# Gated DeltaNet scan: norms, gate rows and the first decays placed between slabs of the projection, the meta tokens' small inverse reordered

## Chip, cores and metric

The kernel runs on one core of a Trainium2 chip. The metric is the device time of one execution in microseconds, as the median of several runs.

## Reference

Two transformer blocks over a sequence of 256 tokens of width 1024, in f32. The first block puts 16 meta tokens (and 112 masked pads) ahead of the sequence and has two layers, of which the first mixes with a gated delta network. The change touches only the following part of it:

- `qkv = silu(conv4(h @ w_qkv))`: a projection to 4096 columns (8 heads of q, 8 of k, 16 of v, 128 each), a causal depthwise convolution of 4 taps, then silu.
- q and k are divided by their l2 norms per head and token: `q * rsqrt(sum(q*q) + eps)`, with a scale of 128^-0.5 for q.
- `beta = sigmoid(...)` and `g = -exp(a_log) * softplus(... + dt_bias)` give a gate per head (16) and token; `G` is the running sum of g inside a chunk.
- For each chunk and head a lower triangular matrix `A = beta * exp(G_i - G_j) * (k_i . k_j)` is inverted (I + A), giving the corrected values; the state S is carried from chunk to chunk, and outputs are `q S * exp(G)` plus a masked `(q_i . k_j)` part.

The kernel takes the 16 meta tokens as a first short chunk (the pads are zero), and the 256 others as two chunks of 128.

## The kernel before

Activations lie features first (128 features by T = 272 tokens, or 256). Weights stream from memory in slabs of 128 x 2048 words into a ring of four, and each slab is split by ACT (`w_hi`, L294) and DVE (`w_lo`, L297) into a high and a low part, two slabs ahead of use; PE makes three fast products per weight block (L411, L412, L413). Each engine has a program of its own, in order; semaphores join them. `each_product` writes ACT's and DVE's part of a streamed phase. It makes a hardware loop of four slabs, unless it is given `between`, a function called ahead of each slab, in which case the phase is written out straight; `stream_pe` does the same on PE. `late` with `lag=2` is work done two output parts behind.

The phase `gdn_qkv` has 16 slabs of two output parts (32 parts of 128 columns). For part u ACT copies the bank twice (L753, and L754 scaled by the last tap), DVE adds the three other taps (L769), and ACT applies silu two parts later (L759). A slab's split is called at its second part, ahead of that part's taps.

Around it stand, in the order of the programs:

- `rows_act`/`rows_dve`, ahead of the projection: the rows beta, G, exp(G) and others, 16 heads on 16 partitions. `rows_pe` (L732) turns them into columns, `cols_dve` copies them (L739, L740) into `colv` and `colb`. Both come after the projection.
- The norms, after the projection: ACT squares q and k in one instruction (L571, 16 heads by 272 tokens), PE sums over the features by 16 products with a one-column mask (L598, two passes each, so 32 records), ACT takes the root (L582), DVE the reciprocal (L587), and POOL sends the rows to memory (L815) and fetches them back on all partitions (L817 for the 16 meta tokens, L933 for a group of heads). The gate rows go the same way (L807, L811, L929).
- `first_dve`, `first_act`, `first_pe`, `first_pool`: the meta tokens' chunk for all 16 heads. DVE normalizes k and q (L830, L831) and makes the decays (L832, L834, exp on ACT L866, L836); PE makes k.k and k.q (L886, L887) and turns k and v (L890, L892); DVE makes A (L840), the masked attention (L841) and the first step of the inverse (L843, L845). Three levels double the block size: POOL masks A (L824), PE makes Y (L904), ACT copies it (L871), PE makes two products (L909, L912), DVE subtracts (L856, L858). Then PE makes the new values (L916), ACT copies them (L874), PE makes the outputs (L920) and after them the state (L923), which DVE and ACT copy to `St0` (L861, L879).
- `ahead_kn`, `ahead_diff` on DVE, `ahead_exp` on ACT, `ahead_beta` on POOL: the same preparation for the first group of four heads (L940, L941, L947, L951, L961, L968). Then `group_*` runs four times, once for each group of four heads, over the two chunks of 128; its first product is L1100, its A is L1007, and `first_turned` (L1116) is PE's first product that needs the result of the group's first DVE steps.

Of the kernel before, what the change touches and what calls it, by code (L numbers as in the profile page):

```python
# [192 lines left out]
def program(nc, x_t, meta_t, mem_t, positions, stream, consts, params, sg_w_t, sg_bias, out_t, counts):  # L193
    with ExitStack() as ctx:
# [415 lines left out]
        sqh = area(rows_at + 9 * T, 16, T)  # L610
# [22 lines left out]
        bc0 = area(2048, 64, META, of=spare)  # L633
# [7 lines left out]
        kn0, qn0 = (spare[:, 6144 + 128 * i:6144 + 128 * (i + 1)].rearrange("p (a b) -> p a b", b=META) for i in range(2))  # L641
# [105 lines left out]
        def qkv_act(act):  # L747
# [12 lines left out]
            each_product(act, "gdn_qkv", 1, project, ACT.Silu, split="hi", late=silu, lag=2)  # L760

        def qkv_dve(dve):
# [8 lines left out]
            each_product(dve, "gdn_qkv", 1, body, split="lo")  # L771
# [17 lines left out]
        def by2(v):  # L789

            return v.rearrange("p (a b) n -> p a b n", b=2)
# [10 lines left out]
        def first_pool(pool):  # L802
# [14 lines left out]
            pool.dma_start(bc0[:, 0:16, :], on_all(scratch, 0, (T, 16), (1, META))).then_inc(S.sem("first_rows_in"), 16)  # L817
            fetch_norm_rows(pool, 0)
# [6 lines left out]

        def first_dve(dve):
            inc = lambda ins, step=None: S.inc(ins, "first_dve", step)
            own = lambda: S.own(dve, "first_dve")
            dve.wait_ge(S.sem("first_rows_in"), 32)
            inc(dve.tensor_tensor(kn0, qkv[:, 8:16, 0:META], bc0[:, 8:16, :], ALU.mult))  # L830
            inc(dve.tensor_tensor(qn0, qkv[:, 0:8, 0:META], bc0[:, 0:8, :], ALU.mult), "kn")  # L831
            inc(dve.tensor_tensor(c0["dec"], bc0[0:META, 32:48, :], over(cn("causal")[0:META, 0:META], HV), ALU.add))  # L832
            own()
            inc(dve.tensor_tensor(c0["dec"], c0["dec"], down(colv[0:META, 0, 1, :], META), ALU.subtract), "diff")  # L834
            dve.wait_ge(*S.at("first_act", "dec"))
            inc(dve.tensor_tensor(c0["decb"], c0["dec"], bc0[0:META, 16:32, :], ALU.mult))  # L836
# [4 lines left out]
            inc(dve.tensor_tensor(by2(c0["attn"]), two(kq), by2(c0["dec"]), ALU.mult), "attn")  # L841
# [4 lines left out]
            dve.wait_ge(*S.at("first_pe", "tok"))  # L846
            for b in range(2):
                kt = two(tile4(ps[b][0:META, :]))
# [1890 lines left out]
```

## Time and profile before

| | |
|---|---|
| median of 3 runs | 1789.52 us (1786.73 to 1790.91) |
| the profiled execution | 1782.2 us, span 1780.5 us |
| mean granted TensorE clock | 0.957 of full |
| busy share of the span | PE 92%, DVE 61%, ACT 46%, POOL 23% |
| projection `gdn_qkv` on PE | 29.0 to 126.3 us |
| first group starts on PE (L1100) | 196.87 us |

Times inside the profile are microseconds from the span's start. PE is the matrix engine and PEld its weight loads, DVE the vector engine, ACT the scalar engine, POOL GpSimd. "Busy" of PE includes records that overlap. The granted clock is a fraction of full speed; it takes two levels here, 0.50 (1.2 GHz) and 1.00 (2.4 GHz), and a stretch shows the mean. "Idle before <- X" names what ended an engine's wait.

### The profile page before, as it was taken

The page shows a single profiled execution, that of the slowest core. Times are in us where ns is not written, and L with a number is a line of the kernel's source. Part 1 is how long each engine was busy: PE and PEld are TensorE (multiplying, and loading weights), DVE is VectorE, ACT ScalarE, POOL GpSimd, SP SyncE. Part 2 cuts the span into 40 slices and gives each one's busy share as a digit, 9 for nine tenths or more (in the row PEclk, how much of TensorE's full clock was granted, in tenths as well). Part 3 has the DMA queues.
Part 4 walks back from the last instruction along what each step waited for, and adds up shares of the span by engine and source line. Part 5 has one row for each costly group of instructions (what it writes and reads, how often), then busy time and mean ns, then how long its engine had stood idle before and what let it go on. Part 6 is the DMA issues. An engine that isn't in the chain of part 4 may idle for free.

```text
span 1780.5 us, 32196 instructions
## 1 busy us (share of the span) xinstructions
PE 1640.7 (92%) x12819; PEld 1555.6 (87%) x12819; DVE 1085.1 (61%) x1519; ACT 827.2 (46%) x1190; POOL 408.4 (23%) x388
## 2 busy tenths in 40 slices
PE   5986888989889999899899998999999899889998
PEld 4984788878889999898899998999988489889998
DVE  4872355535558883575588846665563756566654
ACT  5661344445445544555555545433443145554332
POOL 0001344430024562000246513321100000212210
PEclk9996699999899999999999999999999999999999
DMA  5542011105335544363244455554633443445543
GB/s 216 186 143 62 4 47 50 51 1 193 137 123 169 186 140 154 124 235 119 72 170 185 145 169 193 197 179 147 234 126 119 162 147 119 137 151 202 196 155 128
DMA packets 41400, 252.40 MB, mean 142 GB/s; under 512 B 4480, under 2 KB 6640, under 8 KB 19296
## 3 DMA queue, kind: packets, MB, share of 16 engines
q1 hardware_dynamic: 37376, 233.13, 37.7%
q0 software_dynamic: 3936, 18.05, 3.3%
q8 instruction: 61, 1.00, 0.2%
q14 instruction: 27, 0.22, 0.0%
HBM read 249.99 MB, written 1.17 MB: 141 GB/s over the span
## 4 chain that ended last, share of the span: by engine, by line
PE 81%; DVE 10%; ACT 5%; issue 2%; DMA 1%; POOL 0%; SPq 0%; ACTq 0%; DVEq 0%; POOLq 0%
PE bank L411 20%; PE bank L412 20%; PE bank L413 20%; DVE w_lo L297 3%; PE bank L1124 2%; PE bank L1132 2%; PE bank L415 2%; PE bank L598 2%; ACT w_hi L294 2%; PE bank L542 1%; PE bank L429 1%; PE bank L1139 1%; PE bank L430 1%; PE bank L431 1%; DVE rs L551 1%
## 5 line engine op out<-in xcount | busy, mean ns | idle before, releaser
L411 PE MATMUL bank<-work_r,w_hi 128*128 128x256 f32 (+2 forms) x3264 | 932.5, 286 | 29.9 <-DVE w_lo L297 16.4
L412 PE MATMUL bank<-work_r,w_hi 128*128 128x256 f32 (+2 forms) x3264 | 926.2, 284 | 0.0
L413 PE MATMUL bank<-work_r,w_lo 128*128 128x256 f32 (+2 forms) x3264 | 925.8, 284 | 0.0
L297 DVE TENSOR_TENSOR w_lo<-ring,w_hi 128x2048 fp32r<-128x2048 f32 (+2 forms) x233 | 497.9, 2139 | 331.6 <-ACT w_hi L294 331.5
L411 PEld LDWEIGHTS bank<-work_r,w_hi 128*128 128x128 f32 x3264 | 622.9, 191 | 35.8 <-DVE w_lo L297 22.5
L294 ACT ACTIVATE w_hi<-ring 128x2048 fp32r<-128x2048 f32 (+2 forms) x233 | 408.1, 1754 | 470.6 <-PE bank L413 470.5
L412 PEld LDWEIGHTS bank<-work_r,w_hi 128*128 128x128 f32 x3264 | 622.4, 191 | 0.5
L413 PEld LDWEIGHTS bank<-work_r,w_lo 128*128 128x128 f32 x3264 | 622.1, 191 | 0.0
L1326 POOL TENSOR_TENSOR work<-work 128x272 f32<-128x272 f32 (+1 forms) x44 | 91.6, 2082 | 137.0 <-ACT work L1289 137.0
L523 POOL TENSOR_TENSOR sq<-sq 128x256 f32<-128x256 f32 (+2 forms) x36 | 57.6, 1599 | 268.3 <-ACT sq L500 267.5
L1314 DVE SCALAR_TENSOR_TENSOR work<-work,params_sb 128x272 f32<-128x272 f32 (+1 forms) x176 | 99.8, 608 | 5.2 <-issue 0.2
L429 PE MATMUL bank<-work_r,w_hi 128*128 128x256 f32 (+2 forms) x112 | 41.7, 372 | 16.9 <-DVE work_r L1721 14.9
L1698 POOL CAST work_r<-mix 128x256 f32 (+1 forms) x44 | 17.5, 399 | 164.0 <-DVE mix L1689 164.0
L769 DVE SCALAR_TENSOR_TENSOR work<-work,params_sb 128x272 f32<-128x272 f32 x96 | 46.9, 500 | 10.6 <-ACT work L754 2.8
L1302 DVE TENSOR_TENSOR work<-bank,rs 128x272 f32<-128x272 f32 (+1 forms) x88 | 37.7, 431 | 24.8 <-PE bank L413 24.7
L1026 DVE TENSOR_TENSOR sq<-sq,bank 128x256 f32<-128x256 f32 x48 | 18.0, 417 | 51.5 <-PE bank L1132 51.5
L1282 ACT ACTIVATE work<-work,params_sb 128x272 f32<-128x272 f32 (+1 forms) x88 | 48.1, 595 | 1.3 <-DVE work L1302 1.2
L1710 ACT ACTIVATE work_r<-hs,params_sb 128x256 fp32r<-128x256 f32 (+2 forms) x48 | 24.6, 512 | 51.0 <-DVE hs L1742 21.8
L979 POOL TENSOR_TENSOR sq<-mix,consts_sb 128x512 f32<-128x512 f32 x24 | 33.6, 1400 | 46.1 <-PE bank L1124 28.8
L1330 POOL TENSOR_TENSOR work_r<-work,work_r 128x272 f32 (+3 forms) x44 | 40.1, 910 | 7.7 <-POOL work_r L1328 7.4
L429 PEld LDWEIGHTS bank<-work_r,w_hi 128*128 128x128 f32 x112 | 23.5, 210 | 19.9 <-issue 16.0
L1700 POOL TENSOR_TENSOR work_r<-mix,work_r 128x256 f32 (+1 forms) x44 | 37.5, 853 | 7.5 <-POOL work_r L1698 7.2
(410 smaller groups left out, 1900.9 us busy)
## 6 DMA issues: line engine op xcount, KB each, us to landing
ring<-in_stream SPq DMA_DIRECT2D x166, 1024.0 KB, 4.8
ring<-in_stream SPq DMA_DIRECT2D x64, 704.0 KB, 4.1
ring<-in_stream SPq DMA_DIRECT2D x10, 768.0 KB, 4.3
work<-rows_scratch POOLq DMA_DIRECT2D x4, 1632.0 KB, 7.9
work<-rows_scratch POOLq DMA_DIRECT2D x4, 544.0 KB, 8.7
work<-rows_scratch_o POOLq DMA_DIRECT2D x1, 2176.0 KB, 8.9
ring<-in_stream SPq DMA_DIRECT2D x3, 512.0 KB, 7.2
work<-rows_scratch_m POOLq DMA_DIRECT2D x1, 1088.0 KB, 8.1
```

The lines of the kernel that those rows point to most:

```text
L294: eng.activation(w_hi[:, slot, 0:size], raw_w, ACT.Copy).then_inc(hi_done, 1)
L297: eng.tensor_tensor(w_lo[:, slot, 0:size], raw_w, w_hi[:, slot, 0:size].bitcast(F32), ALU.subtract).then_inc(lo_done, 1)
L411: pe.matmul(out, w_hi[:, slot, at:at + P], hi, start=first, stop=False)
L412: pe.matmul(out, w_hi[:, slot, at:at + P], lo, start=False, stop=False)
L413: mm = pe.matmul(out, w_lo[:, slot, at:at + P], hi, start=False, stop=last)
L429: pe.matmul(out, w_hi[:, slot, at:at + P], hi, start=(k == 0), stop=False)
L523: S.inc(pool.tensor_tensor(sq[:, 0, 0:n], sq[:, 0, 0:n], sq[:, k, 0:n], ALU.add), "square_sums")
L769: S.inc(dve.scalar_tensor_tensor(out=y, in0=r[:, t:t + T], scalar=gdn_taps[:, un.u, t:t + 1], in1=y, op0=ALU.mult, op1=ALU.add), "qkv_dve")
L1282: S.inc(act.activation(y_gu[p2][:, m, 0:w], raw[p2][:, m, 2:w + 2], ACT.Identity, bias=bias[:, un.u, m:m + 1], scale=taps[:, un.u, m, 2:3] ...
L1314: S.inc(dve.scalar_tensor_tensor(out=y, in0=raw[p2][:, m, t:t + w], scalar=taps[:, un.u, m, t:t + 1], in1=y, op0=ALU.mult, op1=ALU.add), " ...
L1326: S.inc(pool.tensor_tensor(h, silu_g[un.j % 2][:, 0:w], y_gu[un.j % 2][:, 1, 0:w], ALU.mult), "up_pool")
L1330: S.inc(pool.tensor_tensor(lo[:, un.u, :], h, hi[:, un.u, :].bitcast(F32), ALU.subtract), "up_pool")
```

## The change

- Squares of q and k are made one head at a time by ACT inside the projection, one behind silu, and PE adds each pair of heads to the sum ahead of slabs 4 to 11. ACT takes the root ahead of slab 12, DVE the reciprocal ahead of slab 13; POOL sends and fetches the meta tokens' norm rows from there.
- The gate rows are turned by PE ahead of slab 3 and copied by DVE ahead of slab 4; the meta tokens' gate rows are fetched as soon as they are stored. The decays are made ahead of slabs 5 (difference), 6 (exp) and 7 (times beta); the normalized k and q of the meta tokens ahead of slab 15.
- `gdn_qkv` is given `between` on PE, ACT and DVE, so it is written out straight on the three.
- In the meta tokens' chunk, k and v are turned between the steps of the inverse, not ahead of it; the masked attention comes after the first step; the state is made ahead of the outputs. The first group's preparation is done ahead of the copies of the state, and PE starts the groups after ACT's copy of the outputs.
- Buffers are moved so that these live at the same time (`sqh`, `bc0`, `kn0`, `qn0`).

```diff
-                pe.wait_ge(S.sem("rown_squares"), (1, 2, 4)[use])
+                pe.wait_ge(S.sem("rown_squares"), (16, 17, 19)[use])
...
-        sqh = area(rows_at + 9 * T, 16, T)
+        sqh = area(8704 + 16 * T, 16, T)
...
-        bc0 = area(2048, 64, META, of=spare)
+        bc0 = sqw[:, 0:64 * META].rearrange("p (a b) -> p a b", b=META)
...
                 S.inc(act.activation(qkv[:, un.u, :], conv_y[:, un.j % 4, :], ACT.Silu), "qkv_act", "silu")
-            each_product(act, "gdn_qkv", 1, project, ACT.Silu, split="hi", late=silu, lag=2)
+                if 1 <= un.u <= 16:
+                    act.wait_ge(*S.at("qkv_act", turn=un.u - 1 + CONV_AHEAD))
+                    rown_squares(act, [(qkv[:, un.u - 1, :], sqh[:, un.u - 1, :])])
+
+            def beside(slab):
+                if slab == 6:
+                    first_decay_act(act)
+                elif slab == 12:
+                    rown_act(act, 0, [], T, 16, cn("l2_scale")[0:16, :], cn("l2_eps"), table=False)
+            each_product(act, "gdn_qkv", 1, project, split="hi", late=silu, lag=2, between=beside)
...
-            each_product(dve, "gdn_qkv", 1, body, split="lo")
+
+            def beside(slab):
+                if slab == 4:
+                    cols_dve(dve)
+                elif slab == 5:
+                    S.own(dve, "cols_dve")
+                    first_diff_dve(dve)
+                elif slab == 7:
+                    first_decay_dve(dve)
+                elif slab == 13:
+                    rown_dve(dve, 0, T, 16)
+                elif slab == 15:
+                    first_keys_dve(dve)
+            each_product(dve, "gdn_qkv", 1, body, split="lo", between=beside)
+
+        def qkv_pe(pe, slab):
+            if slab == 3:
+                rows_pe(pe)
+            for k in (2 * slab - 8, 2 * slab - 7) if 4 <= slab < 12 else ():
+                pe.wait_ge(S.sem("rown_squares"), k + 1)
+                mm = pe.matmul(ps[4][0:16, 0:T], cn("row_of", 15 - k, 16), sqh[:, k, :], start=(k == 0), stop=(k == 15))
+                if k == 15:
+                    S.begin("rown_pe")
+                    S.inc(mm, "rown_pe", "sums")
...
             pool.wait_ge(S.sem("scan_rows_out"), 48)
-            pool.wait_ge(*S.at("cols_dve"))
-            pool.wait_ge(*S.at("qkv_act", turn=31 + CONV_AHEAD))
             pool.dma_start(bc0[:, 16:64, :], on_all(scratch, 16 * T, (T, 48), (1, META))).then_inc(S.sem("first_rows_in"), 16)
-            fetch_gate_rows(pool, 0)
...
             pool.dma_start(bc0[:, 0:16, :], on_all(scratch, 0, (T, 16), (1, META))).then_inc(S.sem("first_rows_in"), 16)
+            pool.wait_ge(*S.at("cols_dve"))
+            pool.wait_ge(*S.at("qkv_act", turn=31 + CONV_AHEAD))
+            fetch_gate_rows(pool, 0)
             fetch_norm_rows(pool, 0)
...
+        def first_keys_dve(dve):
+            dve.wait_ge(S.sem("first_rows_in"), 32)
+            for u in (7, 15):
+                dve.wait_ge(*S.at("qkv_act", turn=u + CONV_AHEAD))
+            S.inc(dve.tensor_tensor(kn0, qkv[:, 8:16, 0:META], bc0[:, 8:16, :], ALU.mult), "first_dve")
+            S.inc(dve.tensor_tensor(qn0, qkv[:, 0:8, 0:META], bc0[:, 0:8, :], ALU.mult), "first_dve", "kn")
...
+                if l == 1:
+                    for b in range(2):
+                        kt = two(tile4(ps[b][0:META, :]))
+                        inc(dve.tensor_tensor(by2(ktl0[0:META, 8 * b:8 * b + 8, :]), kt, by2(down(colv[0:META, 0, 2, 8 * b:8 * b + 8], P)), ALU.mult),
+                            "ktl" if b else None)
+                    values(0)
+                elif l == 2:
+                    values(1)
+            ahead_kn(dve, 0)
+            ahead_diff(dve, 0)
             dve.wait_ge(*S.at("first_pe", "S"))
...
                 inc(mm, f"Y{l}")
+                if l == 1:
+                    keys()
+                elif l == 2:
+                    values(1)
...
                 inc(mm, f"XXT{l}")
+                if l == 1:
+                    values(0)
...
             pe.wait_ge(*S.at("first_act", "vn"))
             for h in range(HV):
+                mm = pe.matmul(ps[h // 4][:, h % 4 * P:(h % 4 + 1) * P], ktl0[0:META, h, :], vb0[0:META, h, :], start=True, stop=True)
+            inc(mm, "S")
+            for h in range(HV):
                 mm = pe.matmul(ps[6][:, h * META:(h + 1) * META], vb0[0:META, h, :], c0["attn"][:, h, :], start=True, stop=True)
             inc(mm, "o")
-            for h in range(HV):
-                mm = pe.matmul(ps[h // 4][:, h % 4 * P:(h % 4 + 1) * P], ktl0[0:META, h, :], vb0[0:META, h, :], start=True, stop=True)
-            inc(mm, "S")
...
             pe.wait_ge(*S.at("first_dve", "S"))
-            pe.wait_ge(*S.at("first_act", "S"))
+            pe.wait_ge(*S.at("first_act", "o"))
...
-            stream_pe(pe, "gdn_qkv", a_parts(0, T), T)
-            rows_pe(pe)
-            rown_pe(pe, 0, lambda k: sqh[:, k, :], 16, 1, T, 16)
+            stream_pe(pe, "gdn_qkv", a_parts(0, T), T, between=lambda slab: qkv_pe(pe, slab))
```

## Rows read from the trace of the kernel before

**Rows 1.** The page of the kernel before, its chain of waits by engine.

```profile
PE 81%; DVE 10%; ACT 5%; issue 2%; DMA 1%; POOL 0%; SPq 0%; ACTq 0%; DVEq 0%; POOLq 0%
```

**Rows 2.** Stretches: length, busy us (instructions) of PE, PEld, DVE, ACT, POOL, clock, DMA.

```profile
80.00:100.00 20.00, 20.00 (x164) 20.00 (x163) 17.32 (x24) 14.17 (x26) 0.00 (x0) 1.00 0.53 189
...
171.00:194.00 23.00, 20.88 (x96) 18.23 (x96) 0.00 (x0) 2.40 (x5) 0.00 (x0) 0.50 0.00 1
...
770.00:790.00 20.00, 20.00 (x164) 19.84 (x163) 10.80 (x15) 6.26 (x5) 1.66 (x3) 1.00 0.60 214
```

**Rows 3.** The chain of waits, 126 to 153 us: start, us, what.

```profile
126.44 0.40 ACT work L753
...
128.86 0.44 ACT work L759
...
133.20 9.60 PE bank L598 x32
...
142.82 0.58 ACT rrow L582
...
143.43 1.85 DVE rrow L587
```

**Rows 4.** The chain of waits, 147 to 205 us.

```profile
147.53 4.47 DMA w_spare<-rows_scratch
...
153.68 1.81 PE bank L890 x8
...
171.01 7.02 PE bank L916 x32
...
178.05 2.03 ACT work L874 x4
...
180.12 7.00 PE bank L920 x32
187.13 7.03 PE bank L923 x32
...
200.72 0.70 DVE mix L1007
...
204.19 0.67 PE bank L1116 x4
```

**Rows 5.** Timeline of ACT and DVE in mid projection: start, us, instruction, idle before.

```profile
84.92 1.92 ACT L294 ACTIVATE w_hi<-ring 128x2048 fp32r<-128x2048 f32 x1 [1.86 <-PE bank L413]
...
90.84 1.92 ACT L294 ACTIVATE w_hi<-ring 128x2048 fp32r<-128x2048 f32 x1 [1.86 <-PE bank L413]
...
104.63 2.29 DVE L297 TENSOR_TENSOR w_lo<-ring,w_hi 128x2048 fp32r<-128x2048 f32 x1 [0.22 <-ACT w_hi L294]
```

**Rows 6.** Groups by line in the projection: count, busy us, mean ns, idle before.

```profile
L769 DVE SCALAR_TENSOR_TENSOR work<-work,params_sb 128x272 f32<-128x272 f32 x95 | 46.4, 500 | 10.6 <-ACT work L754 2.8 <-DVE work L769 0.3 <-issue 0.2
...
L297 DVE TENSOR_TENSOR w_lo<-ring,w_hi 128x2048 fp32r<-128x2048 f32 x14 | 32.0, 2289 | 2.2 <-ACT w_hi L294 2.2
...
L759 ACT ACTIVATE work<-work 128x272 f32 x24 | 10.4, 432 | 0.0
...
L732 PE MATMUL bank<-consts_sb,work 16*128 16x16 f32 x8 | 0.6, 208 | 0.0
```

**Rows 7.** The norm sums of L598 alone, columns as in Rows 2.

```profile
138.00:142.00 4.00, 4.00 (x19) 1.71 (x18) 1.00 0.78 321
```

**Rows 8.** Timeline of all engines, 143 to 197 us.

```profile
143.41 1.28 ACT L1201 ACT_TABLE_LOAD   x1
...
144.71 1.06 ACT L956 ACTIVATE work<-work 128x1024 f32<-128x1024 f32 x1
...
154.29 0.41 DVE L840 TENSOR_TENSOR mix<-bank,mix 16x256 f32<-16x256 f32 x1
...
159.48 0.95 PE L904 MATMUL bank<-mix 16*16 16x16 f32 x32 [0.51 <-issue]
...
196.87 2.07 PE L1100 MATMUL bank<-work 128*128 128x128 f32 x8 [2.73 <-DVE work L941]
```

More of the change, by code:

```diff
@@ L640, in program @@
               for i, n in enumerate(("dec", "decb", "A0T", "attn", "X", "XT", "Am", "Y"))}
-        kn0, qn0 = (spare[:, 6144 + 128 * i:6144 + 128 * (i + 1)].rearrange("p (a b) -> p a b", b=META) for i in range(2))
+        kn0, qn0 = (sqw[:, 1024 + 128 * i:1024 + 128 * (i + 1)].rearrange("p (a b) -> p a b", b=META) for i in range(2))
         obc = area(8704, HV, T)
@@ L824, in first_pool, with first_diff_dve, first_decay_dve @@
                 inc(pool.tensor_tensor(c0["Am"], c0["A0T"], over(lvl[0:META, l, 0:META], HV), ALU.mult), f"Am{l}")
+        def first_diff_dve(dve):
+            dve.wait_ge(S.sem("first_rows_in"), 16)
+            S.inc(dve.tensor_tensor(c0["dec"], bc0[0:META, 32:48, :], over(cn("causal")[0:META, 0:META], HV), ALU.add), "first_dve")
+            S.own(dve, "first_dve")
+            S.inc(dve.tensor_tensor(c0["dec"], c0["dec"], down(colv[0:META, 0, 1, :], META), ALU.subtract), "first_dve", "diff")
+        def first_decay_dve(dve):
+            dve.wait_ge(*S.at("first_act", "dec"))
+            S.inc(dve.tensor_tensor(c0["decb"], c0["dec"], bc0[0:META, 16:32, :], ALU.mult), "first_dve", "decb")
+        def first_keys_dve(dve):
[4 more added lines that the diff above has]
+            S.inc(dve.tensor_tensor(qn0, qkv[:, 0:8, 0:META], bc0[:, 0:8, :], ALU.mult), "first_dve", "kn")
         def first_dve(dve):
@@ L828, in first_dve @@
             own = lambda: S.own(dve, "first_dve")
[L829 to L836, printed above, removed]
             own()
@@ L888, in first_pe, with keys, values @@
             inc(mm, "kq")
-            for h in range(HQ):
-                pe.transpose(ps[h // 4][0:META, h % 4 * P:(h % 4 + 1) * P], kn0[:, h, :], ident)
-            for h in range(HV):
-                mm = pe.transpose(ps[2 + h // 4][0:META, h % 4 * P:(h % 4 + 1) * P], qkv[:, 16 + h, 0:META], ident)
-            inc(mm, "tok")
+            def keys():
+                pe.wait_ge(*S.at("qkv_act", turn=31 + CONV_AHEAD))
+                for h in range(HQ):
+                    mm = pe.transpose(ps[h // 4][0:META, h % 4 * P:(h % 4 + 1) * P], kn0[:, h, :], ident)
+                inc(mm, "ktok")
+            def values(half):
+                for h in range(8 * half, 8 * half + 8):
+                    mm = pe.transpose(ps[2 + h // 4][0:META, h % 4 * P:(h % 4 + 1) * P], qkv[:, 16 + h, 0:META], ident)
+                inc(mm, f"vtok{half}")
             pe.wait_ge(*S.at("first_dve", "XT0"))
@@ L913, in first_pe @@
                 inc(mm, f"XXT{l}")
+                if l == 1:
+                    values(0)
             pe.wait_ge(*S.at("first_dve", f"XT{L0 - 1}"))
@@ L1193, in scan_dve @@
             first_dve(dve)
-            ahead_kn(dve, 0)
-            ahead_diff(dve, 0)
             with dve.Fori(0, GROUPS - 1) as g:
@@ L2401, in _ @@
             qkv_dve(dve)
-            cols_dve(dve)
-            rown_dve(dve, 0, T, 16)
-            S.own(dve, "cols_dve")
             scan_dve(dve)
```

28 lines of the change are left out of this document (13 added, 15 removed).

## Prediction

> **What bounds the kernel.** I read first the page's chain of waits. It runs over PE for 81% of the span [rows 1], so work on PE, and waits of PE, are what count. The stretches then show two kinds of time. In the projection PE is busy for all of its 20.00 us at clock 1.00, with DVE close behind at 17.32 [rows 2]. Between the end of the projection and the first group PE idles, or works at clock 0.50, as in 171 to 194 us [rows 2]. The chain tells who holds the end there. The last slab's last product ends near 126.3 us, ACT copies it from 126.44, and the last silu ends at 129.3 [rows 3]. Then squares, sums, root, reciprocal and a trip through memory follow one another until 152.0 [rows 3, 4]; the inverse leads to L916 at 171.01, and three blocks of about 7.0 us on PE with a copy of 2.03 between them end at 194.2. The first group's A starts at 200.72 and PE's first product behind it at 204.19 [rows 4]. Everything after 204.19 keeps its order, so the time gained is the move of that one product. I measure it from the projection's end, called E (126.3 before): it stands at E+77.9.
>
> **Part 1: the projection grows.** PE gets 16 sums of two passes. The old block has 32 records in 9.60 us [rows 3], part of it at half clock. At clock 1.00 it issues 18 loads in 4.00 us [rows 7], 0.22 each; 32 of them cost 7.2 us. The 12 small transposes, of which 8 take 0.6 us [rows 6], about 0.8 in all, stood behind E under ACT's and DVE's tail, and now lie on PE's path. Sum: 8.0 us.
>
> Is PE still the one that sets the pace? A slab lasts 5.92 us (84.92 to 90.84). Three slabs behind the first of these the w_hi at 102.68 starts as a slab ends (84.92 + 3 x 5.92); its w_lo starts at 104.63 and ends at 106.9; the slab that needs it starts at 102.6 + 5.92 = 108.5: 1.5 us to spare. ACT idles 1.86 us a slab, DVE 0.22 [rows 5]. DVE's own work is one w_lo of 2.29 and six taps of 0.50, some 5.6 with their gaps [rows 5, 6].
>
> In slabs 4 to 11 PE's two sums stretch the slab by 0.9 us. That gives DVE room for what it gets there: two differences and decb of 16x256 (0.41 each, as L840 in [rows 8]), and six copies of up to 128x48, which are smaller (estimate 0.7 in all, at most 6 x 0.41). It gives ACT room for two squares a slab (0.4 each, by L759 [rows 6]) and for exp with two table loads (0.41 + 2 x 1.28, the load by [rows 8]): I count ACT 1 us late at most in slab 6, inside the 1.5. Cost: 0.
>
> In slab 12 the stretching is over. Root and two loads cost ACT 0.58 + 2.56 = 3.1 us [rows 3, 8], against 1.86 idle; w_hi of slab 14 is 1.3 to 1.9 us late against 1.5 to spare, which just fits. Behind it the reciprocal, 1.85 us [rows 3], stands ahead of w_lo of the last slab, which also finds its second part's copies late. Following the three queues item by item, I get that w_lo ready 1.1 us after PE wants it. Taken: 1.1 us. The projection grows by 9.1 us. From below the growth is 8.0. From above, if everything given to ACT (16 x 0.4 + 1.0 + 4 x 1.28 = 12.5) and to DVE (0.7 + 1.2 + 1.85 + 0.5 = 4.3) came through, it is 8.0 + 16.8 = 24.8.
>
> The trace shows no pause around a table load: the one at 143.41 takes 1.28 us and the next instruction starts 0.02 us after it [rows 8]. The Trainium skill ("ScalarE: Activation LUTs", What ACT_TABLE_LOAD costs) adds a drain of about 1.38 us, 2.66 us in all for each switch of set, and tells the author to do all functions of one set together, which the new order does not. By that price each pair of loads costs 5.3 us, the last two splits come about 2.8 us later, and the gain shrinks from 18 to about 15. This trace does not agree with that price; the measured one is used.
>
> **Part 2: what goes from behind E.** Squares, sums, root, reciprocal, both trips and the normalizing leave the path. The norm rows now take 6.7 us (from the reciprocal's end at 145.28 to 152.0 [rows 3, 4]) beside the last slabs. Between the reciprocal and `first_keys` DVE has one w_lo and the taps of four parts, 2.2 + 4 x 1.7 = 9 us, so some 2 us are to spare. The gate rows have tens of us. DVE's last taps end 2.5 us behind E before; with the reciprocal and keys ahead of them I count 3.1. A of the meta tokens starts there, at E+3.1, where before it started at 154.29 [rows 8], E+28.0: 24.9 us gained.
>
> **Part 3: the inverse in its new order.** A, Y and XT take 1.3: E+4.4. PE's turn of X ends at E+5.0, but ACT has silu to E+3.55, the table load (1.28) and the v copy (1.06 [rows 8]) until E+5.9, so X is copied by 6.3. POOL issues two fetches behind that silu and has until 6.3 for them and the mask. Y1 at 6.35. From here eight turns of keys or values cost 1.8 us at half clock (L890 [rows 4]), and each small product block 1.0. PE's queue is then Y1, keys, XX1, XXT1, values, which ends at 12.9; Y2, values, XX2, XXT2 at 17.6; a subtraction (0.4), Y3, copy, XXT3, a subtraction: L916 at E+21.15. DVE's scalings of keys and values fit in those waits. From A to L916 is 18.05 us against 16.7 before (154.29 to 171.01): 1.3 lost, because the turns of values, once under the DVE steps, now stand between the levels. Bounds: 14.8 us if the turns hide (3.3 to Y1, and the 11.5 from L904 to L916 before [rows 4, 8]), 20.2 if all three add their 1.8 to that.
>
> **Part 4: outputs and state.** L916 to the end of the two blocks stays 23.2 us (171.01 to 194.18) in either order. PE then starts the group after ACT's copy of the outputs, 0.5, where it waited 2.7 before (194.18 to 196.87 [rows 8]) for DVE's copies and `ahead_kn`: 2.2 gained. The rest of the preparation is done by then, so A of the group waits for PE alone, and `first_turned` for PE's 6.0 us of products, where before DVE had it wait 7.3 (196.87 to 204.19): 1.4 gained. Bounds for both: 0 and 5. New position: 21.15 + 23.2 + 0.5 + 6.0 = E+50.8.
>
> **Sum.** 24.9 - 1.3 + 2.2 + 1.4 gives 27.1 behind E; less 9.1, the gain is 18.0 us. The profiled execution would go from 1782.2 to 1764.2 us. The median before is 1789.52, 7.3 above that execution; I take the same difference off it: **1771.5 us**.
>
> **Rivals.**
>
> *The splits become the bound.* ACT and DVE do not catch up, every load and every inserted item adds to the lateness, and PE waits in many slabs. For it: DVE's idle of 0.22 us a slab. Against it: the 0.9 us that PE gives back in slabs 4 to 11. Growth 13 to 24.8 in place of 9.1 gives a gain of 2 to 14, so 1776 to 1787 us; in the middle 1781.
>
> *The clock stays up.* The idle 26 us ahead of the inverse are gone, so L916, L920 and L923 could meet clock 1.00 and take 3.5 in place of 7.0 each: 10.5 more, a gain of 28.5, 1761 us. Against it: those three blocks kept PE busy for 20.88 of 23 us, and the clock stayed at 0.50 throughout [rows 2]. They use 16 rows of the array, and the work ahead of them would again be mostly such work. The Trainium skill ("TensorE: Matmul & The Clock Gate", What's actually happening) says that activity releases the throttle; for these small products the trace does not agree.
>
> *Code written out straight.* The phase leaves its hardware loop on three engines, and PE runs 768 products from fresh code. Were each 24 ns slower, 18 us would be lost and the gain with it; at 40 ns the kernel is 13 us slower, 1802 us. It decides from 24 ns on a pitch of 123. Against it: `ml_in` is written out with `between` too, and shows 164 records in 20 us of full PE, the same 164 as the looped projection [rows 2].
>
> *Loads that cost double.* With a pause behind each table load as long as the load, the last two pairs add 2.6 us in slabs 12 to 14, where nothing is left to spare: a gain of 15.4, 1774 us. Against it: the 0.02 us above [rows 8]. The drain that the Trainium skill ("ScalarE: Activation LUTs", What ACT_TABLE_LOAD costs) states would be such a pause.
>
> *The norm rows come late.* Then DVE waits ahead of slab 15 with the last taps behind it, and every us beyond the spare 2 costs one. The streamed weights share the DMA engines there, which they did not at 145 us. A doubling of the 6.7 would cost 5 us: 1776.5.
>
> **Chances.** Gain of 13 to 23 us as forecast 0.71; loads at double 0.05; splits bound 0.09; late rows 0.05; clock up 0.06; written-out code, or another loss that eats all, 0.03; nothing won or lost 0.01. About 0.2%, 3.6 us, is what a measurement can tell from no change here. Faster 0.96, same 0.02, slower 0.02. The range takes in the forecast's own bounds (Part 3's 14.8 to 20.2, Part 4's 0 to 5, Part 1's 8.0), late rows and the nearer half of the splits' case: 1763 to 1781 us.
>
> **What would show it.** In the new profile: PE busy throughout slabs 4 to 13, with each of these up to 11 about 6.8 us long; one wait of PE for w_lo of about 1 us ahead of the last slab; the projection's end near 135.4; the meta tokens' first products right there, A about 3 us behind; the three 7 us blocks from 156.5, at clock 0.50; the first group on PE near 180 and `first_turned` near 186. The forecast is wrong if PE waits for w_lo in many slabs, if DVE waits for the norm rows, if the 7 us blocks shorten, or if the order of levels and turns leaves PE idle beyond the 18 us counted.

## The result and the profile after

The changed kernel takes 1762.82 us, median of four runs (1758.42 to 1764.79), against 1789.2 us for the kernel before in the same measurement. The ratio is 0.9847 with a 95% interval of 0.983 to 0.9865. The forecast was 1771.5 us with a range of 1763 to 1781, so the time lies 0.18 us under the range; three later timings of the same kernel, 1764.35, 1763.94 and 1768.0 us, lie inside it. The profiled execution took 1764.79 us, with a span of 1763.1; the forecast for the profiled execution was 1764.2. Between the two profiled spans the gain is 17.4 us (1780.5 to 1763.1) where 18.0 was forecast; between the two medians it is 26.4. Both halves of this need an explanation: where the 17.4 come from, and what the other 9 are.

The page's chain of waits by engine, the answer to [rows 1]:

```profile
PE 80%; DVE 9%; ACT 5%; issue 2%; DMA 2%; POOL 0%; SPq 0%; ACTq 0%; DVEq 0%; POOLq 0%
```

Three stretches of the kernel after, with the columns of [rows 2]. The second is the one with the three 7 us blocks, which lay at 171 to 194 before.

```profile
80.00:100.00 20.00, 20.00 (x148) 17.55 (x146) 15.70 (x22) 12.84 (x28) 0.00 (x0) 1.00 0.44 151
...
158.00:181.00 23.00, 20.39 (x96) 17.89 (x95) 5.55 (x9) 4.14 (x8) 2.49 (x2) 0.50 0.00 1
770.00:790.00 20.00, 20.00 (x166) 19.84 (x165) 14.96 (x26) 11.88 (x17) 0.00 (x0) 1.00 0.46 170
```

In the projection (first row) PE is still busy for all 20 us at clock 1.00. Its records fell from 164 to 148 because the sums, counted among them, and the pause behind them take longer than split products. The three blocks still run at 0.50. In the third row, from a phase that the change does not touch, PE keeps its pace (166 records against 164); the window lies some 17 us further on in the program than in [rows 2], so the work of the other engines in it differs.

The chain of waits of the kernel after, from the reciprocal to `first_turned` (start, us, what), answers to [rows 3] and [rows 4]. In this kernel's numbering L778 is the taps (before L769), L872 the normalized keys, L963 the product Y, L946 the turning of the keys, L983, L987, L990 the new values, the state and the outputs (before L916, L923, L920), L1167 the group's first product (L1100) and L1183 `first_turned` (L1116).

```profile
126.36 1.76 DVE rrow L587
...
128.41 1.67 DMA rows_scratch<-rrow
...
130.37 6.60 DMA sq<-rows_scratch
...
136.99 0.29 DVE sq L872
...
140.49 0.44 ACT work L759
...
143.88 1.03 PE bank L963 x32
144.91 1.80 PE bank L946 x8
...
158.51 7.02 PE bank L983 x32
...
165.55 2.03 ACT work L926 x4
...
167.62 7.19 PE bank L987 x32
174.81 6.65 PE bank L990 x32
...
181.49 0.39 ACT work L932
...
182.32 2.07 PE bank L1167 x8
...
187.08 0.45 PE bank L1183 x4
```

The meta tokens' first products on PE (L939) start at 137.89, so E is 137.8. The steps read, measured from E: L983 at E+20.7 (before E+44.7), L1167 at E+44.5 (before E+70.6), L1183 at E+49.3 (before E+77.9). So 28.6 us are gained behind E, the projection grows by 11.5, and 17.1 remain at `first_turned`; the span has 17.4.

The waits in the projection of the kernel after, 38 to 140 us (engine, line waited for, us in total, times, longest):

```profile
PEld bank L411 <- issue: 3.6, 8, 0.5
...
PE bank L411 <- DVE w_lo L297: 2.5, 2, 1.9
...
DVE sq L872 <- DMA sq<-rows_scratch: 0.8, 1, 0.8
```

PE waits twice in these 102 us for a `w_lo`: 1.9 us at the projection's start, which the kernel before has as well (one wait, 1.9 us), and 0.53 ahead of the last slab. The first line is new: eight pauses of PE's weight loads of 0.45 us, one in each slab that carries sums. The timeline of PE in one such slab:

```profile
85.30 0.62 PE L800 MATMUL bank<-work,consts_sb 128*16 128x272 f32 x2
85.85 0.39 PE L411 MATMUL bank<-work_r,w_hi 128*128 128x272 f32 x1
```

and ACT's splits, whose spacing is the pace of the slabs:

```profile
85.00 1.91 ACT L294 ACTIVATE w_hi<-ring 128x2048 fp32r<-128x2048 f32 x1 [1.52 <-PE bank L413]
...
92.14 1.91 ACT L294 ACTIVATE w_hi<-ring 128x2048 fp32r<-128x2048 f32 x1 [1.52 <-PE bank L413]
```

A slab with two sums lasts 7.14 us, against 5.92 in [rows 5]. A pair of sums costs 1.22 us, and not the 0.9 forecast.

The timeline of ACT around the root, and behind the last silu (the last two rows):

```profile
116.49 1.28 ACT L582 ACT_TABLE_LOAD   x1
117.78 0.57 ACT L582 ACTIVATE rrow<-bank,consts_sb 16x272 f32<-16x272 f32 x1
118.26 0.37 ACT L753 ACTIVATE work<-bank 128x272 f32<-128x272 f32 x1
...
119.02 1.28 ACT L759 ACT_TABLE_LOAD   x1
120.31 0.43 ACT L759 ACTIVATE work<-work 128x272 f32<-128x272 f32 x1
...
140.94 1.28 ACT L1266 ACT_TABLE_LOAD   x1
142.24 1.06 ACT L1023 ACTIVATE work<-work 128x1024 f32<-128x1024 f32 x1
```

Behind each table load of 1.28 us the next instruction starts 0.01 to 0.02 us later.

### The profile page after: what moved, and what is told of

It reads as the page before. It is cut to its first block, busy times and chain, and to the rows that moved or that the text cites. A ratio compares the mean times of both kernels' runs of the same rounds, so it can differ in the third digit from the quotient of the medians.

```text
span 1763.1 us, 31930 instructions
## 1 busy us (share of the span) xinstructions
PE 1636.0 (93%) x12819; PEld 1551.5 (88%) x12819; DVE 1086.4 (62%) x1519; ACT 832.0 (47%) x1208; POOL 409.2 (23%) x388
## 3 DMA queue, kind: packets, MB, share of 16 engines
q0 software_dynamic: 3936, 18.05, 3.3%
## 4 chain that ended last, share of the span: by engine, by line
PE 80%; DVE 9%; ACT 5%; issue 2%; DMA 2%; POOL 0%; SPq 0%; ACTq 0%; DVEq 0%; POOLq 0%
PE bank L411 20%; PE bank L412 20%; PE bank L413 20%; DVE w_lo L297 3%; ACT w_hi L294 2%; PE bank L1191 2%; PE bank L415 2%; PE bank L1199 2%; PE bank L598 1%; DMA work<-rows_scratch 1%; PE bank L542 1%; PE bank L429 1%; PE bank L430 1%; PE bank L431 1%; PE bank L1206 1%
## 5 line engine op out<-in xcount | busy, mean ns | idle before, releaser
L429 PE MATMUL bank<-work_r,w_hi 128*128 128x256 f32 (+2 forms) x112 | 41.4, 370 | 17.1 <-DVE work_r L1785 14.9
L1366 DVE TENSOR_TENSOR work<-bank,rs 128x272 f32<-128x272 f32 (+1 forms) x88 | 37.7, 430 | 25.4 <-PE bank L413 25.3
L778 DVE SCALAR_TENSOR_TENSOR work<-work,params_sb 128x272 f32<-128x272 f32 x96 | 46.9, 499 | 2.5 <-ACT work L754 0.2
```

Source lines behind the costliest of these rows:

```text
L429: pe.matmul(out, w_hi[:, slot, at:at + P], hi, start=(k == 0), stop=False)
L778: S.inc(dve.scalar_tensor_tensor(out=y, in0=r[:, t:t + T], scalar=gdn_taps[:, un.u, t:t + 1], in1=y, op0=ALU.mult, op1=ALU.add), "qkv_dve")
```

## Experiments

"Gain" is always the difference to the kernel before. The ratios are of runs taken in turns on one chip, with their 95% intervals.

### The code written out straight, and nothing else

```diff
-            each_product(dve, "gdn_qkv", 1, body, split="lo")
+            each_product(dve, "gdn_qkv", 1, body, split="lo", between=lambda slab: None)
```

and the same for ACT's `each_product` and PE's `stream_pe`.

> The kernel before with the projection written out straight on PE, ACT and DVE, nothing else. Theory A (the gain came from the moves alone): same as before within 0.1%. Theory B (the hardware loops of the projection cost time in most executions, more than in the profiled one): faster by 5 to 9 us, which would be the part of the gain that the forecast missed. Rival (fresh code costs): slower.

Measured: 1784.16 us (1778.15 to 1794.96, 12 runs), ratio 0.999 (0.9967 to 1.0014). Slabs last 5.92 us, as in the loop, and from the start of slab 4's split to the meta tokens' first product pass 103.0 us, against 103.2 to 103.4 in the profiles of the kernel before. So the profile shows no cost of the straight code; the timing alone would leave room for 2.5 us lost or 5.9 gained. One row moves, the six taps of DVE:

```profile
91.63 3.06 DVE L769 SCALAR_TENSOR_TENSOR work<-work,params_sb 128x272 f32<-128x272 f32 x6
```

They take 3.06 us where the loop's take 3.49 (records of the kernel before at 89.08). It is a slack that this kernel does not need, since PE sets the pace. Whether DVE needs it for the new work in the changed kernel is not shown by a run.

### The two halves alone

`order_only` has the new order of the inverse, of state and outputs, and of the first group's preparation; the norms, gate rows and decays stay behind the projection. `moves_only` has everything that goes into the projection, with the old order behind it. Each was timed twice, on two chips, to see how far a gain repeats.

```diff
  order_only, against the changed kernel: first_dve has the moved steps again
+            first_keys_dve(dve)
+            first_diff_dve(dve)
+            first_decay_dve(dve)
...
  moves_only, against the changed kernel: first_pe, first_dve, first_act and scan_* have the old order
-                if l == 1:
-                    keys()
-                elif l == 2:
-                    values(1)
...
+            pe.wait_ge(*S.at("qkv_act", turn=31 + CONV_AHEAD))
+            for h in range(HQ):
```

> The kernel before with the new order in the meta tokens' chunk alone (inverse first, turns between its levels, state ahead of outputs, first group's preparation ahead of the copies); the projection and the norms as before. By the forecast's parts 3 and 4: 1.3 lost, 3.6 gained, so 2.3 us faster; if the missed gain of some 8 us lies in the new order (a clock level that rises for the blocks of outputs and state), 8 to 12 us faster.

> The changed kernel with the old order in the meta tokens' chunk (k and v turned ahead of the inverse, outputs ahead of the state, preparation behind). By the forecast's parts 1 and 2: 24.9 less 9.1, 15.8 us faster than before; by the profile after, whose projection grew by 11.5, 13.4 us. If the missed gain lies in the moves, 22 us or more.

> The new order in the meta tokens' chunk alone, again. By its first run 3 to 4 us faster than before; theory A: the same here.

> The moves into the projection alone, again. By its first run 13.8 us faster than before (ratio 0.9926); theory A: the same here, and with order_second the sum of both halves is the change's own gain on this chip.

| | median us (range, runs) | ratio (interval) | span |
|---|---|---|---|
| order_only | 1781.35 (1775.85 to 1788.44, 12) | 0.9984 (0.9967 to 1.0001) | 1783.3 |
| order_second | 1780.73 (1774.59 to 1785.19, 12) | 0.9961 (0.9943 to 0.9978) | 1777.8 |
| moves_only | 1771.87 (1770.38 to 1776.03, 6) | 0.9926 (0.9909 to 0.9942) | 1770.1 |
| moves_second | 1769.65 (1765.32 to 1780.15, 6) | 0.9912 (0.9885 to 0.9939) | 1763.6 |

The moves bring 13.2 and 15.7 us by ratio, the order 2.9 and 7.0. The positions in the profiles (us) are steadier, and show where each half works:

| start of | before | order_only | moves_only | after |
|---|---|---|---|---|
| first products of the meta tokens | 152.6 | 153.0 | 137.9 | 137.9 |
| new values (L916) | 171.0 | 171.7 | 158.0 | 158.5 |
| first group on PE (L1100) | 196.9 | 195.5 | 183.9 | 182.3 |
| `first_turned` (L1116) | 204.2 | 200.6 | 191.2 | 186.9 |
| end of `up1` | 1014.8 | 1011.7 | 1001.2 | 997.6 |

From the first products to the new values the new order takes 20.6 us in the changed kernel, and the old order 20.1 in `moves_only`. So coming first with the inverse gains nothing by itself. The chain of waits of `moves_only` shows the old order (L934 and L936 turn keys and values, L894 and L896 scale them, L948 is Y, L960 the new values):

```profile
141.02 1.79 PE bank L934 x8
142.81 2.67 PE bank L936 x16
...
151.04 1.02 PE bank L948 x32
...
158.00 7.02 PE bank L960 x32
...
174.11 7.03 PE bank L967 x32
181.16 1.29 DVE w_spare L906 x2
```

The old order starts its inverse 7.2 us later (Y at 151.04 against 143.88), and then runs through it without turns between the levels, which cost 3 x 1.80 in the new one. The order's gain of 4.3 us (191.2 to 186.9; these are starts of records, and the chain counts the last one from 187.08, where the product before it ends) arises behind the new values: 33.2 us from there to `first_turned` in `moves_only`, 28.4 in the changed kernel. About 1.5 us of it hang on when the clock comes back to 1.00: in `after_again` and `after_cut` it comes back later, and there the order gains 2.7 us up to `first_turned`, counted from the start of slab 4's split.

### The outputs ahead of the state again

```diff
             for h in range(HV):
+                mm = pe.matmul(ps[6][:, h * META:(h + 1) * META], vb0[0:META, h, :], c0["attn"][:, h, :], start=True, stop=True)
+            inc(mm, "o")
+            for h in range(HV):
                 mm = pe.matmul(ps[h // 4][:, h % 4 * P:(h % 4 + 1) * P], ktl0[0:META, h, :], vb0[0:META, h, :], start=True, stop=True)
             inc(mm, "S")
-            for h in range(HV):
-                mm = pe.matmul(ps[6][:, h * META:(h + 1) * META], vb0[0:META, h, :], c0["attn"][:, h, :], start=True, stop=True)
-            inc(mm, "o")
...
-            pe.wait_ge(*S.at("first_act", "o"))
+            pe.wait_ge(*S.at("first_act", "S"))
```

> The changed kernel with the outputs made ahead of the state again, ACT's copies in the old order and PE starting the groups behind the state's copy; the preparation stays ahead. By part 4 the group's start then waits for ACT's two copies of the state (1.1 us) where it waited for one small copy (0.5): 0.6 us slower than the changed kernel. If the order of the two blocks itself carried the 2.2 us of part 4, 2 us slower.

Measured: 1767.44 us (1762.28 to 1773.43, 6), ratio 0.9886 (0.9856 to 0.9917), against 0.9877 (0.9845 to 0.9909) for the changed kernel beside it: not told apart by time. In the profile the new values to the group's first product take 24.8 us instead of 23.8. The timeline of `outputs_first` shows the wait:

```profile
182.76 1.29 DVE L911 COPY w_spare<-bank 128x512 f32<-128x512 f32 x2 [19.29 <-PE bank L990]
...
184.39 1.85 PE L1167 MATMUL bank<-work 128*128 128x128 f32 x7 [1.66 <-DVE w_spare L911]
```

PE stands 1.66 us for DVE's two copies of the state, against 0.86 for ACT's single copy of the outputs in the changed kernel. So of the 2.05 us gained in this stretch, about 1.0 comes from the swap, and the rest from the preparation that is done ahead.

### Where the projection's excess growth comes from

Two theories stood for the 1.22 us of a pair of sums. A: each change from split products to sums and back costs 0.3 us, whatever number of sums stands between. B: each sum costs more than [rows 7] says.

```diff
-            for k in (2 * slab - 8, 2 * slab - 7) if 4 <= slab < 12 else ():
+            for k in {5: range(0, 4), 7: range(4, 8), 9: range(8, 12), 11: range(12, 16)}.get(slab, ()):
```

`sums_early` has `{6: range(0, 8), 10: range(8, 16)}`, the root and the reciprocal beside slab 10 instead of 12 and 13, and the keys ahead of slab 14 instead of 15.

> The changed kernel with four sums ahead of slabs 5, 7, 9 and 11 in place of two ahead of each of slabs 4 to 11. The profile after shows slabs of 7.13 us where 5.92 + 0.92 was forecast, so a pair costs 1.22. Theory A (0.3 us is the price of each change between the split products and the f32 sums): four changes in place of eight, the projection 1.2 us shorter. Theory B (each sum costs 0.6 wherever it stands): the same length.

> The changed kernel with eight sums ahead of slab 6 and eight ahead of slab 10, the root and the reciprocal beside slab 10, the normalized k and q ahead of slab 14. Two changes on PE in place of eight save 1.8 us by theory A of the run before; the lateness behind the reciprocal (0.5 us of PE ahead of the last slab) and DVE's wait for the norm rows (0.8) go too. Expected 2 to 3 us faster than the changed kernel; none of it if sums cost the same in any place and DVE's lateness comes from its own pace.

The pauses of PE's loads, in `sums_by_four`:

```profile
PEld bank L411 <- issue: 1.8, 4, 0.5
```

and in `sums_early`:

```profile
PEld bank L411 <- issue: 0.9, 2, 0.5
```

The pause is 0.45 us each time that a run of sums ends, eight times in the changed kernel, four and two times here. From the start of slab 4's split to the meta tokens' first product pass 88.3 us in the changed kernel (in all five of its profiles), 87.05 in `sums_by_four` and 85.6 in `sums_early` (and in both its repetitions). Four runs of sums less save 1.2, that is 0.3 each. Six less should save 1.9, and the wait of 0.53 us for the last `w_lo` is gone too: 2.4 of the 2.7. A holds: 0.3 us for each run of sums. By time, 1765.61 us (0.9879, 0.9845 to 0.9913) and 1767.71 (0.9889, 0.986 to 0.9918) are not to be told from the changed kernel's 1764.35 beside them.

### The same two kernels again

> The kernel before, unchanged: a second profiled execution. The first took 1782.2 us, the unprofiled ones 1786.7 to 1790.9. Theory A (executions of this program differ, and the first profile is of a quick one): this execution takes some 1785 to 1790 us, and the extra lies in one or a few stretches that the two profiles of one program show. Theory B (profiled executions are always quicker than timed ones, by some 7 us): again 1782 us with the same stretches.

> The changed kernel, unchanged, in more rounds. The profiles of five kernels show that the phases with 256 columns (down1, up2, up3, down3) each run at one of two paces in an execution (a slab of up2 in 5.44 or 5.66 us, of a down phase in 3.74 or 3.89), whatever the kernel. Theory A (the change is worth the 17.4 us of the two profiles, and the rest of the 26 us was which paces the few timed executions drew): ratio 0.990 to 0.991, 16 to 18 us. Theory B (the change moves the later phases into the quick pace): 22 to 27 us, and all four phases quick in the new profile again.

> The kernel before, unchanged, timed against itself and profiled once more. Ratio 1.000 within its interval; a spread of some 20 us between single executions. In the profile the stretch up to the end of up1 (first block's last phase with 258 columns) ends at 1015 us within 1 us, as in its two other profiles; what differs lies behind it, in the phases with 256 columns, by their pace.

> The changed kernel beside the kernel before on one chip with the two halves of the change. Theory A (the change is worth what the stretch up to up1 shows, 16 to 18 us; the 26 us of the first timing, with four executions of each, drew the other paces): ratio 0.990 to 0.991 here. Theory B (something of the change makes the later phases quicker): 22 us or more, ratio under 0.988, and more than the sum of the two halves.

| | median us (range, runs) | ratio (interval) | span |
|---|---|---|---|
| before_again | 1786.19 (1 run) | | 1784.5 |
| before_third | 1790.04 (1781.71 to 1794.46, 12) | 1.0012 (0.9994 to 1.003) | 1791.1 |
| after_again | 1764.35 (1761.51 to 1769.5, 5) | 0.9877 (0.9845 to 0.9909) | 1759.8 |
| after_third | 1763.94 (1761.56 to 1770.96, 6) | 0.988 (0.9856 to 0.9904) | 1759.8 |

The kernel before runs anywhere from 1778.2 to 1799.04 us within one set of 23 runs. Its profiles show one reason. A stretch of `up2` in the kernel before:

```profile
1120.00:1140.00 20.00, 20.00 (x179) 20.00 (x178) 13.19 (x16) 8.35 (x7) 6.38 (x11) 1.00 0.52 178
```

and the same stretch in `before_again`, the identical program:

```profile
1120.00:1140.00 20.00, 20.00 (x172) 20.00 (x172) 13.65 (x14) 7.26 (x8) 10.48 (x11) 1.00 0.52 185
```

Both have PE busy for all 20 us at clock 1.00, one with 179 products, the other with 172. ACT's splits in the first:

```profile
1143.76 1.92 ACT L294 ACTIVATE w_hi<-ring 128x2048 fp32r<-128x2048 f32 x1 [3.22 <-PE bank L413]
...
1149.20 1.92 ACT L294 ACTIVATE w_hi<-ring 128x2048 fp32r<-128x2048 f32 x1 [3.22 <-PE bank L413]
```

and in the second:

```profile
1140.99 1.92 ACT L294 ACTIVATE w_hi<-ring 128x2048 fp32r<-128x2048 f32 x1 [3.43 <-PE bank L413]
...
1146.64 1.92 ACT L294 ACTIVATE w_hi<-ring 128x2048 fp32r<-128x2048 f32 x1 [3.43 <-PE bank L413]
```

A slab of 48 products lasts 5.44 us in one and 5.65 in the other: 113.3 or 117.8 ns for a product of 256 columns. One pace holds for a whole phase, and the next phase of the same execution can have the other. At 118 ns `up2` takes some 4.2 us more, `up3` 4.7, `down3` 2.1; `down1` takes both paces too. The phases `gdn_qkv`, `gdn_z`, `up0` and `ml_in` with 272 columns (5.92 us a slab) and `up1` with 258 (5.80) have a single pace in all profiles. The changed kernel has both paces too; one execution (`after_fourth`) with `up2` at 113 ns and `up3` at 118:

```profile
1120.00:1140.00 20.00, 20.00 (x179) 20.00 (x178) 13.12 (x15) 8.89 (x8) 4.55 (x8) 1.00 0.60 210
...
1600.00:1620.00 20.00, 20.00 (x172) 20.00 (x172) 12.97 (x15) 8.54 (x8) 4.55 (x8) 1.00 0.57 205
```

Over all profiles of whole kernels, `up2`, `up3` and `down3` ran at 118 ns in 8 of 21 cases without the moves and in 7 of 30 with them, which doesn't tell the two groups apart.

### The two kernels without the later phases

To take the later phases out of the comparison, both kernels end behind `gdn_out` and store the first mixer's output.

```diff
-            phase_read(sp, "down3")
-            sp.dma_start(out_t.rearrange("(k p) t -> p k t", p=P), h2)
+            mix_was_read(sp, "gdn_out")
+            sp.dma_start(out_t.rearrange("(k p) t -> p k t", p=P), mix[:, :, 0:SEQ])
...
             evac_mix_act(act, "gdn_out", T)
+            return
```

> The kernel before, ended behind the phase gdn_out: all phases with 256 columns are left out, and what is stored is the first mixer's output in place of the result. Some 530 us. Theory A (the spread of the whole kernel comes from the phases with 256 columns): single executions within 6 us of each other in place of 20, the rest from when the first loads land and from the clock's level in the groups.

> The changed kernel, ended behind gdn_out in the same way (it leaves out the same work). Theory A (the change's own gain is what its own stretch shows, and the rest of the 23 us between the medians comes from the paces of the later phases): 16.5 to 18 us less than before_cut. Theory B (the profiles miss part of the change's own gain, which timed executions have): 22 to 24 us less.

> The kernel of sums_early, ended behind gdn_out in the same way. Its profile shows the projection 2 to 2.6 us shorter than in the changed kernel, but the whole kernel was timed 4 us slower. Theory A (paces again): 2 us less than after_cut here. Theory B (it really is slower): more than after_cut.

| | median us (range, 5 runs) | gain on before_cut |
|---|---|---|
| before_cut | 526.7 (526.17 to 531.8) | |
| after_cut | 510.65 (509.29 to 511.5) | 16.05 |
| sums_early_cut | 505.59 (505.1 to 507.71) | 21.1 |

Here the ranges are narrow, and the change is worth 16.05 us by the medians and 17.2 by the means of five runs (527.6 and 510.4; one run of `before_cut` is 5 us above the other four). That is nearer to the forecast's 18.0 and the first profiles' 17.1 than to the 26.4 of the first timing. It doesn't put the rest of the gain behind `gdn_out`, though: in the whole kernels' profiles the same stretch, up to the first slab of `up0`, gains 19 us on average (between 537.2 and 542.5 us before, 519.5 and 522.2 after). The next section says where.

Of the 5.06 us between the last two, 2.6 are the shorter projection. Another part is the start: slab 4's split starts at 52.47 in `after_cut` and at 49.70 in `sums_early_cut`, as the first weights arrive. That differs between executions of one program too (49.60, 49.81, 51.92 and 52.25 in the four whole profiles of the changed kernel), so it isn't put down to `sums_early`.

### sums_early and the changed kernel on one chip

> The kernel before once more, for its profile: theory A (paces fall by chance) and theory B (they follow the program) both allow any of the two paces here; a slow pace in at least one of up2, up3 and down3, as in two of its three profiles, is the likelier.

> The variant that was 5.1 us faster than the changed kernel when both ended behind gdn_out, whole again. Theory A (which paces the later phases take falls by chance in each execution): over both calls it should come out 3 to 5 us faster than the changed kernel, some 1759 us. Theory B (a program has its own odds of the slow paces, and this one has worse ones): again 1765 to 1769 us, and a slow pace in at least one of up2, up3, down3 of its profile.

> The changed kernel beside it on the same chip, with a fourth profile. Theory A: about 1763 to 1768 us, and the paces may be slow. Theory B: 1763 us, all three phases quick as in its three other profiles.

`before_fourth`: 1783.94 us in one run, span 1782.2. `sums_early_second`: 1762.21 (1758.32 to 1765.54, 6), ratio 0.9865 (0.9835 to 0.9895). `after_fourth`: 1768.0 (1762.17 to 1770.63, 6), ratio 0.989 (0.986 to 0.992). This turns the order of the earlier comparison, where the changed kernel had 1764.35 and `sums_early` 1767.71. The profile of `sums_early_second` drew 113 ns in all three phases, that of `after_fourth` 118 in `up3` and `down3`. Over all their runs the two have the same mean (1764.9 us in 12 runs of `sums_early`, 1765.0 in 21 of the changed kernel). Whole kernels therefore don't settle which of the two is faster; the cut ones say `sums_early`, by 2.6 us in the profile and 5.1 in time.

## Why the prediction was right about the change and wrong about the time

**How large the gain is.** The timings on record hold 93 executions of the kernel before, with a mean of 1787.3 us, and 21 of the changed kernel, with a mean of 1765.0. They differ by 22.2 us, with a 95% interval of 1.8 either way if the runs are taken as independent. By ratio the four timings give 27.3, 22.0, 21.5 and 19.7 us. So the forecast gain of 18.0 was 4.2 too small. The rest of the 8.7 us between 1771.5 and 1762.82 is the luck of few runs: the three timings before (median 1789.52) lay 2.3 above the mean of the 93, and the four of the changed kernel 2.2 below the mean of the 21.

**The step that failed** is the premise on which the sum rests: "Everything after 204.19 keeps its order, so the time gained is the move of that one product". The product moved as forecast (17.1 us against 18.0), and the order behind it is kept. But the time behind it is not: it was put at nothing without a row for it. The next table counts from the start of slab 4's split, which leaves out when the first weights arrive (us; the lowest and highest of the profiles; `before_cut` and `after_cut` are taken in, and `straight` with the kernel before):

| up to | before (6 profiles) | order_only (2) | moves_only (2) | after (5) |
|---|---|---|---|---|
| meta tokens' first product | 103.0 to 103.4 | 103.2 to 103.3 | 88.3 | 88.3 |
| `first_turned` | 154.5 to 155.0 | 150.6 to 150.9 | 141.5 | 137.2 to 138.8 |
| split at the end of `gdn_z`'s first slab | 368.6 to 372.6 | 365.2 to 365.7 | 355.0 to 355.6 | 348.5 to 351.7 |
| of this, `first_turned` to the second group | 45.6 to 48.8 | 46.4 | 45.8 | 44.8 |

At `first_turned` the change has gained 17.0 us by the means, at the third row 19.6. The first two profiles, 368.6 and 351.7, are the pair that lies closest together in that row, so they hid it. A part of the 2.7 us is seen in the first group. The timeline of the kernel before has PE waiting for `first_turned`:

```profile
204.19 0.66 PE L1116 MATMUL bank<-consts_sb,sq 128*128 128x128 f32 x4 [1.36 <-DVE sq L1011]
```

and these are the 10 us from its start, and the whole first group from there, in the kernel before and in the changed one (columns of [rows 2]):

```profile
204.19:214.19 10.00, 8.55 (x52) 7.38 (x53) 5.11 (x9) 3.98 (x10) 7.05 (x4) 0.83 0.01 2
204.19:249.84 45.65, 42.33 (x329) 38.73 (x330) 22.08 (x42) 19.91 (x36) 21.73 (x16) 0.96 0.15 50
...
186.92:196.92 10.00, 7.89 (x61) 6.72 (x60) 5.49 (x9) 4.53 (x11) 7.09 (x5) 1.00 0.00 0
186.92:231.72 44.80, 40.81 (x331) 37.20 (x329) 21.97 (x42) 19.90 (x36) 21.70 (x16) 1.00 0.15 51
```

In the kernel before, the clock is at 1.00 from 203 to 205 us, around this wait, and at 0.50 from 206 to 209; the 10 us have a mean of 0.83. So it is in all eight profiles with the old order of the meta tokens' chunk (`straight` and `moves_only` too), each with such a wait of 1.3 to 1.6 us; in the twelve with the new order PE doesn't wait there and the mean is 1.00. A mean of 0.83 means 3.4 us at 0.50, which cost at most half of that, 1.7 us. That the fall comes from the wait was not tested. The other part, some 1 us, differs from profile to profile and has no known cause, and the same holds for what lies between the 19.6 us and the 22.2 of the timings.

**The last step of the sum.** "The median before is 1789.52, 7.3 above that execution; I take the same difference off it". The 7.3 us are chance: the profiled 1782.2 lies 5.1 below the mean of the 93, with the pace of 113 ns in `up2`, `up3` and `down3`. Without this step the sum gives 1764.2, only 1.4 from 1762.82, but that would have been luck: a start 5.1 us too low and a gain 4.2 us too small nearly cancel.

**The phases behind.** In the profiles of each kernel (before 1780.5, 1784.5, 1791.1, 1782.2; after 1763.1, 1759.8, 1759.8, 1768.9) the mean spans differ by 21.7. Up to the end of `up1` it is 19.3 (1014.8, 1015.4, 1019.1, 1020.0 against 997.6, 999.6, 998.0, 996.8). Behind it the two groups overlap (762.2 to 772.0 us before, 760.2 to 772.1 after). The paces fall differently in each execution and explain much of this scatter. What sets a pace was not found, and an influence of the changed program on it is not excluded.

**Part 1.** Growth 11.5 us against 9.1. The sums are the term that was mis-sized: 16 of them cost 8 x 1.22 = 9.8 where 7.2 was taken. [Rows 7] shows sums in one unbroken run; placed between split products, each run costs 0.3 us more. PE remained the bound: the last `w_lo` came 0.53 us late (forecast 1.1). ACT's root with its two loads and DVE's reciprocal (1.83) behaved as counted.

**Part 2.** Right: 25.4 us against 24.9. DVE's A (L881) starts at 140.38, E+2.6, forecast E+3.1. The norm rows took longer: from the reciprocal's end at 128.13 to 136.97 are 8.8 us against 6.7, since the fetch lasted 6.60 in place of the 4.47 of [rows 4]. They used up the 2 us spare, and DVE waited 0.82 us for them ahead of slab 15. It didn't reach PE in full, as the last silu still came at E+3.1.

**Part 3.** A to the new values took 18.13 us, forecast 18.05: 1.4 lost against 1.3. The queue went as written, Y at 143.88, keys, two products, values.

**Part 4.** L983 to L1167 took 23.81 us against 25.86 before, 2.05 gained (forecast 2.2). From L1167 to L1183 passed 4.76 us, not the forecast 6.0: 2.6 gained in place of 1.4, because in this execution the clock came back to 1.00 within the stretch. In `after_again`, where it didn't, the same stretch took 6.1. Of the four whole profiles of the changed kernel three have the shorter stretch. The term holds within its bounds.

**The sum** of these, 25.4 - 1.4 + 2.05 + 2.6 = 28.6, less 11.5, is 17.1. Two errors, of 2.4 and 1.5 us, in opposite directions, nearly cancel.

**The rivals.** *The splits become the bound*: no, one wait of 0.53 us. *The clock stays up*: no; in the second row of the stretches above it is 0.50, with the 7 us blocks as long as before. *Code written out straight*: nothing lost (ratio 0.999). *Loads at double*: no, the instruction behind a load starts at once. The Trainium skill's drain of about 1.38 us ("ScalarE: Activation LUTs", What ACT_TABLE_LOAD costs) is not seen here either, at three table loads between 116 and 143 us. *Late norm rows*: true in kind, 0.8 us on DVE where 5 was priced.

## What to carry to other kernels

A forecast made from one profiled execution needs several profiles of each kernel beside it: here the first two drew the smallest difference of all pairs behind the changed part, and the distance of one execution to the median was chance. Measure the stretches that keep their order too, since a clock level at their start can change with what stands ahead of them. When single executions scatter by 20 us, cut the kernel behind the changed part: the runs then scattered by 2 to 6 us. When small foreign products go between the products of a full PE, put them there in few long runs: every run costs a fixed amount besides its products.

## What was not expected of the hardware

Products of 256 columns run at 113.3 or at 117.8 ns each (slabs of 5.44 or 5.65 us), constant through a phase, at the same granted clock of 1.00, in the same program; those of 272 columns in `gdn_qkv`, `gdn_z`, `up0` and `ml_in` only at 123.3 (5.92 us). The granted clock came back to 1.00 at the first group and fell again behind a wait of PE of 1.36 us (mean of 0.83 over the next 10 us), in every profile with the old order and in none with the new. A run of f32 sums onto 16 columns, put between split products, costs 0.3 us beyond the sums, and shows as a pause of 0.45 us of the weight loads behind it. And a table load of 1.28 us let the next instruction start 0.01 to 0.02 us later at the three places looked at.
